# Weight-quarter sums of a Strassen-like MLP moved from VectorE to accumulating DMAs of GpSimd's queue

## The chip, the cores and the metric

The kernel runs on one core of a Trainium2 chip. The metric is the device time of one execution in microseconds (us); a median of several runs is given. A profile is one execution recorded by the hardware profiler, and the rows quoted below come from it. TensorE is called PE there, VectorE DVE, ScalarE ACT, GpSimd POOL, and SP is the engine from whose queue the loads are issued.

## What is computed

Two layers of a hybrid encoder work on 640 tokens (512 of a prompt, 128 of eight running streams) with a width of 1024. The part that matters here is the MLP at the end of each layer; its hidden width is 4096, and all is float32:

```python
h2 = rms_norm(x, ln2_w)
x = x + jnp.square(jax.nn.relu(h2 @ w_up)) @ w_down
```

## The kernel before

**Two-part products.** Every float32 operand of a matmul is split into a high and a low part, and a product is three matmuls (high by high, high by low, low by high). For a weight, ACT copies the raw floats into the reduced type (the high part, `weight_half` at L1119 to L1133), then DVE subtracts that from the raw floats (the low part, `weight_half` at L1772 to L1776).

**Seven products for eight.** The MLP is cut into four blocks of 1024 hidden features, in each layer. A block has an up stage and a down stage, so there are 16 such stages ("quads") in the two layers. In a quad the weights are a 2 by 2 arrangement of quarters, 11, 12, 21 and 22, each 512 by 512 floats (1 MB). Instead of the eight products of quarters for the prompt's tokens, seven products are made (a Winograd form of Strassen's scheme), with these weights, in this order: item 0 is 11, item 1 is 21, item 2 is 11 + 12, item 3 is 11 + 12 + 22, item 4 is 12 + 22, item 5 is 22, item 6 is 11 + 12 + 22 + 21. The code calls them B11, B21, SUM_1112, SUM_111222, SUM_1222, B22, SUM_ALL. The 128 stream tokens need plain products, which ride on items 0, 1, 4 and 5 (`up_sample`, `down_sample`): behind the item's own matmuls in general, but ahead of them for item 4, and in the down stage for item 5 too.

**Slots and ring.** The raw quarters lie in four 1 MB slots, `raws`. Each quarter is loaded once by a DMA from SP's queue (`load_quarter`, L453 to L457). The sums are made in place: DVE adds 12, then 22, then 21 onto the slot of 11, and 22 onto the slot of 12 (`weight_sum`, L1778 to L1798). An item has two halves, h0 and h1 of 512 KB each, and each half is summed, split and released by itself, so DVE makes 8 sums per quad. The split halves go into `ring`, which has room for two items: item n takes the place of item n - 2, half by half.

**Order.** Each engine works through a queue written out by hand. For item n, half h: ACT waits until PE is through with that half of item n - 2 and until the weight sum is there, and makes the high part; DVE makes the low part; PE waits for the low part. The next sum onto the same slot may only be made when DVE has read the slot for that low part. DVE's queue also holds the additions of PE's results into `x` (`add_to_x`, L1821), the sums of hidden parts (L1807), and the differences and low parts of the activations (`a_difference`, L1847 to L1856; `a_item_lo`, L1840). ACT's queue also holds copies from PSUM, ReLU and squares, and the high parts of the activations (L1221). In an up stage, two of these (`read_back`, L1195 and L1197) stand between the high parts of the two halves of item 4. GpSimd does nothing in the MLP beyond five small root computations ahead of it and two behind.

Of the kernel before, what the change touches and what calls it, by code (L numbers as in the profile page):

```python
# [17 lines left out]
DEPTH, D, TOK, SEQ, NB, NS = 2, 1024, 640, 512, 8, 16  # L18
P = 128
# [97 lines left out]
SLOTS = [(0, 1, 2, 3), (2, 3, 1, 0), (1, 0, 3, 2), (3, 2, 0, 1)]  # L117


def slot_of(quad, name):  # L120

    return SLOTS[quad % 4][("11", "12", "21", "22").index(name)]

# [3 lines left out]
SUMS = [(SUM_1112, 0), (SUM_1112, 1), (SUM_111222, 0), (SUM_111222, 1), (SUM_1222, 0), (SUM_1222, 1), (SUM_ALL, 0),  # L127
        (SUM_ALL, 1)]


def sums_to(quad, product, half):
    return quad * len(SUMS) + SUMS.index((product, half)) + 1

# [53 lines left out]
def program(nc, x_p, x_s, state_ret, state_conv, norm_rows, ln2_w, w_in, conv_w, ret_w, w_out, w_up, w_down,  # L187
# [6 lines left out]
    with ctx:  # L194
# [78 lines left out]
        sample_hidden = place("sample_hidden", [P, 2, 512], f32)  # L273
# [24 lines left out]
        tail = place("tail", [P, FT, 2 + 2 * NB], f32)  # L298
# [63 lines left out]
        slot_in = [Signal(f"slot_in{s}", 16 * QUADS) for s in range(4)]  # L362
# [3 lines left out]
        weights_summed = Signal("weights_summed", QUADS * len(SUMS))  # L366
# [72 lines left out]
        def settle(eng):  # L439


            eng.sem_inc(waits_passed, 1)
# [3 lines left out]
        def _(sp):  # L446
# [46 lines left out]
            with sp.Fori(0, DEPTH) as layer:  # L493
# [46 lines left out]
                for name in ("11", "21", "12", "22"):  # L540
                    load_quarter(layer, 0, name)
                sp.wait_ge(xn_ready.sem, xn_ready.at(layer, 2 * NT))
                load_norm_row(norm_rows, layer + 1)
                for quad in range(1, QUADS):
                    first = (quad - 1) * PRODUCTS
                    sp.wait_ge(weights_summed.sem, weights_summed.at(layer, sums_to(quad - 1, SUM_ALL, 1)))
                    settle(sp)
                    load_quarter(layer, quad, "11")
                    sp.wait_ge(half_lo.sem, half_lo.at(layer, 2 * (first + SUM_1222) + 2))
                    settle(sp)  # L550
                    load_quarter(layer, quad, "21")
                    sp.wait_ge(half_lo.sem, half_lo.at(layer, 2 * (first + B22) + 2))
                    settle(sp)
                    load_quarter(layer, quad, "12")
                    sp.wait_ge(half_lo.sem, half_lo.at(layer, 2 * (first + SUM_ALL) + 2))
                    settle(sp)
                    load_quarter(layer, quad, "22")
                sp.wait_ge(step_done.sem, step_done.at(layer, STEP["up", NBLK - 1, SUM_ALL, 1] + 1))
# [364 lines left out]
        def _(act):  # L923
# [89 lines left out]
            with act.Fori(0, DEPTH) as layer:  # L1013
# [105 lines left out]
                def weight_half(item, h):  # L1119
                    quad, i = divmod(item, PRODUCTS)  # L1120
                    if i in (B11, B21, B22):
                        slot = slot_of(quad, RAW_OF[i])
                        act.wait_ge(slot_in[slot].sem, slot_in[slot].at(layer, 16 * (quad + 1)))
                    else:
                        act.wait_ge(weights_summed.sem, weights_summed.at(layer, sums_to(quad, i, h)))
# [223 lines left out]
        def _(pool):  # L1349

# [80 lines left out]
            with pool.Fori(0, DEPTH) as layer:  # L1431
# [27 lines left out]
                for t in range(NT):  # L1459
                    row_rstd(layer, NT, t)  # L1460
                for p in range(2):
                    row_rstd(layer + 1, 0, p)
# [7 lines left out]
        def _(dve):  # L1470
# [173 lines left out]
            with dve.Fori(0, DEPTH) as layer:  # L1644
# [133 lines left out]
                def weight_sum(quad, i, h):  # L1778

                    a, b = {SUM_1112: ("11", "12"), SUM_111222: ("11", "22"), SUM_1222: ("12", "22"),  # L1780
                            SUM_ALL: ("11", "21")}[i]
                    if i == SUM_1112:
                        slot = slot_of(quad, "12")
                        dve.wait_ge(slot_in[slot].sem, slot_in[slot].at(layer, 16 * (quad + 1)))
                    elif i == SUM_111222:
                        slot = slot_of(quad, "22")
                        dve.wait_ge(slot_in[slot].sem, slot_in[slot].at(layer, 16 * (quad + 1)))
                    before = {SUM_1112: B11, SUM_111222: SUM_1112, SUM_ALL: SUM_111222}
                    if i in before:
                        dve.wait_ge(half_lo.sem, half_lo.at(layer, 2 * (quad * PRODUCTS + before[i]) + h + 1))  # L1790
                    if i == SUM_ALL:
                        dve.wait_ge(half_lo.sem, half_lo.at(layer, 2 * (quad * PRODUCTS + B21) + h + 1))
                    else:
                        n = SUMS.index((i, h)) + quad * len(SUMS)
                        if i in (SUM_111222, SUM_1222):
                            dve.wait_ge(weights_summed.sem, weights_summed.at(layer, sums_to(quad, SUM_1112, h)))
                    out = raw_half(quad, a, h)
                    nc.vector.tensor_tensor(out, out, raw_half(quad, b, h), ALU.add).then_inc(weights_summed.sem, 1)  # L1798

# [91 lines left out]
                def up(b):  # L1891
                    q, item = 2 * b, 2 * b * PRODUCTS
# [5 lines left out]
                    weight_sum(q, SUM_1112, 0)  # L1898
# [3 lines left out]
                    weight_sum(q, SUM_1112, 1)  # L1902
# [5 lines left out]
                    weight_sum(q, SUM_111222, 0)  # L1908
# [6 lines left out]
                    weight_sum(q, SUM_111222, 1)  # L1915
# [142 lines left out]
```

## Time and profile before

| | |
|---|---|
| median of 3 runs | 1522.8 us (1522.54 to 1523.48) |
| the profiled execution: time, span | 1517.21 us, 1515.4 us |
| PE busy, share of the span | 1433.9 us, 95% |
| DVE busy | 947.2 us, 63% |
| ACT busy | 593.2 us, 39% |
| POOL busy | 131.6 us, 9% |
| mean granted clock of PE | 0.979 |
| read from HBM | 115.83 MB |
| time that packets of SP's queue took, share of 16 DMA engines | 24.0% |

The span is what lies between the first and the last recorded instruction; the profiled execution's own time is 1.8 us more, and the median of the unprofiled runs is another 5.6 us more. Busy shares are averages over a whole program with stages of different kinds. What an edit is worth in the MLP is read from who waits for whom there.

### The profile page before, as it was taken

How to read it: one execution, taken by the hardware profiler on the slowest of the kernel's cores; microseconds unless marked ns; L12 is line 12 of the kernel's file. 1: busy time of each engine (PE TensorE's matmuls, PEld its weight loads, DVE VectorE, ACT ScalarE, POOL GpSimd, SP SyncE). 2: the span in 40 equal slices, each digit the busy share in tenths (PEclk: the TensorE clock that was granted, in tenths of full speed). 3: DMA queues.
4: the chain of work that ended last, by engine and by line, in shares of the span. 5: the costliest groups of instructions: out<-in, count | busy, mean ns of one | idle time of the engine just before them, and what ended most of it. 6: DMA issues, size and time to landing. Idle time of an engine off the chain costs nothing.

```text
span 1515.4 us, 22275 instructions
## 1 busy us (share of the span) xinstructions
PE 1433.9 (95%) x8198; PEld 1265.7 (84%) x8198; DVE 947.2 (63%) x1152; ACT 593.2 (39%) x743; POOL 131.6 (9%) x153
## 2 busy tenths in 40 slices
PE   8999999989899899899899999999899999999996
PEld 6888999889689788698688889988887887987985
DVE  6247335396866866867762562535877677677676
ACT  5212222264345345345442113214543543543553
POOL 2433000000000000000043330000000000000001
PEclk9999999999999999999999999999999999999998
DMA  7323111303203303304042221203113213203201
GB/s 254 126 84 113 63 56 57 112 15 112 96 17 112 111 1 112 111 16 153 2 148 97 88 81 63 93 25 121 72 41 111 73 40 111 84 28 112 87 26 70
DMA packets 74677, 124.72 MB, mean 82 GB/s; under 512 B 3332, under 2 KB 20868, under 8 KB 74568
## 3 DMA queue, kind: packets, MB, share of 16 engines
q1 hardware_dynamic: 74424, 123.18, 24.0%
q8 instruction: 70, 1.15, 0.3%
q14 instruction: 39, 0.32, 0.1%
q10 hardware_dynamic: 144, 0.07, 0.0%
HBM read 115.83 MB, written 7.41 MB: 81 GB/s over the span
## 4 chain that ended last, share of the span: by engine, by line
PE 77%; DVE 12%; issue 6%; ACT 4%; POOL 0%; DVEq 0%; DMA 0%; ACTq 0%; POOLq 0%
PE bank L612 22%; PE bank L770 15%; PE bank L622 11%; PE bank L863 11%; PE bank L784 7%; PE bank L876 5%; DVE raws L1798 4%; DVE ring L1775 3%; ACT ring L1132 3%; DVE x L1821 2%; PE bank L662 2%; DVE a_ring L1840 2%; PE bank L700 1%; PE bank L707 1%; PE bank L681 1%
## 5 line engine op out<-in xcount | busy, mean ns | idle before, releaser
L1132 ACT ACTIVATE ring<-raws 128x1024 fp32r<-128x1024 f32 x220 | 231.1, 1055 | 372.6 <-DVE raws L1798 124.3
L1775 DVE TENSOR_TENSOR ring<-raws,ring 128x1024 fp32r<-128x1024 f32 x220 | 268.8, 1222 | 169.2 <-ACT ring L1132 168.3
L863 PE MATMUL bank<-ring,a_ring 128*128 128x512 f32 x1344 | 318.1, 394 | 17.5 <-DVE a_ring L1840 17.5
L770 PE MATMUL bank<-mlp_in_hi,ring 128*128 128x256 f32 x1728 | 320.0, 283 | 0.0
L863 PEld LDWEIGHTS bank<-ring,a_ring 128*128 128x128 f32 x1344 | 254.1, 190 | 74.1 <-issue 20.8
L770 PEld LDWEIGHTS bank<-mlp_in_hi,ring 128*128 128x128 f32 x1728 | 272.1, 191 | 1.4
L770 PE MATMUL bank<-mlp_in_lo,ring 128*128 128x256 f32 x864 | 244.0, 282 | 0.0
L770 PEld LDWEIGHTS bank<-mlp_in_lo,ring 128*128 128x128 f32 x864 | 165.0, 191 | 1.4
L1798 DVE TENSOR_TENSOR raws<-raws 128x1024 f32<-128x1024 f32 x128 | 155.7, 1217 | 0.0
L1359 POOL TENSOR_SCALAR var<-sums 128x1 f32<-128x1 f32 x25 | 9.7, 386 | 1216.4 <-ACT xn L946 1212.8
L622 PE MATMUL bank<-norm_hi,ring 128*128 128x320 f32 x512 | 114.5, 310 | 0.0
L876 PE MATMUL bank<-ring,sample_mid_hi 128*128 128x512 f32 x256 | 88.6, 430 | 25.2 <-DVE ring L1775 25.2
L612 PE MATMUL bank<-ring,norm_hi 128*128 128x512 f32 x320 | 101.6, 399 | 4.2 <-ACT ring L934 2.3
L612 PE MATMUL bank<-pair_a,norm_hi 128*128 128x512 f32 x320 | 100.9, 397 | 0.0
L784 PE MATMUL bank<-ring,sample_in_hi 128*128 128x512 f32 x240 | 81.8, 424 | 18.7 <-DVE ring L1775 18.7
L1821 DVE TENSOR_TENSOR x<-x,bank 128x512 f32<-128x512 f32 x128 | 81.9, 679 | 19.7 <-PE bank L876 16.0
L876 PEld LDWEIGHTS bank<-ring,sample_mid_hi 128*128 128x128 f32 x256 | 53.1, 210 | 40.4 <-DVE ring L1775 28.6
L622 PEld LDWEIGHTS bank<-norm_hi,ring 128*128 128x128 f32 x512 | 86.0, 188 | 0.1
L622 PE MATMUL bank<-norm_lo,ring 128*128 128x320 f32 x256 | 79.1, 309 | 0.0
L612 PEld LDWEIGHTS bank<-ring,norm_hi 128*128 128x128 f32 x320 | 59.5, 191 | 16.4 <-ACT ring L934 2.5
L784 PEld LDWEIGHTS bank<-ring,sample_in_hi 128*128 128x128 f32 x240 | 47.2, 206 | 29.1 <-DVE ring L1775 20.3
L612 PEld LDWEIGHTS bank<-pair_a,norm_hi 128*128 128x128 f32 x320 | 58.9, 188 | 12.3 <-issue 1.0
(179 smaller groups left out, 2092.9 us busy)
## 6 DMA issues: line engine op xcount, KB each, us to landing
raws<-in_w_mlp_up SPq DMA_DIRECT2D x32, 1024.0 KB, 7.3
raws<-in_w_mlp_down SPq DMA_DIRECT2D x32, 1024.0 KB, 7.1
w_raw<-in_w_in SPq DMA_DIRECT2D x28, 1024.0 KB, 5.4
w_raw<-in_w_out SPq DMA_DIRECT2D x8, 1024.0 KB, 5.0
past_state<-in_state_ret SPq DMA_DIRECT2D x8, 512.0 KB, 5.1
out_ret_s<-past_state SPq DMA_DIRECT2D x8, 512.0 KB, 4.9
x<-in_x_prompt SPq DMA_DIRECT2D x4, 512.0 KB, 12.5
norm_row<-in_norm_rows SPq DMA_DIRECT2D x3, 512.0 KB, 3.6
```

The costliest lines, as they stand in the source:

```text
L612: mm = pe.matmul(out, act[a][:, k, tile * P:(tile + 1) * P], w_of(b, n), start=(n == 0 and m == 0), stop=(n == len(ks) - 1 and m == 2))
L622: mm = pe.matmul(out, w_of(chunk, k // 4, a)[:, k % 4, ft * P:(ft + 1) * P], norms[b][:, k, half * HALF:(half + 1) * HALF], start=(k == 0 ...
L662: mm = pe.transpose(out[:, i * P:(i + 1) * P], src[i], identity)
L770: mm = pe.matmul(cols, item_half(item, h, a)[:, k, n * P:(n + 1) * P], mlp_in[i][c][:, k], start=(i in (B11, B21, SUM_1112) and (n, k, m) ...
L784: mm = pe.matmul(out, x5[a][:, k], w[c][:, :, k], start=(i in (B11, SUM_1222) and (k, m) == (0, 0)), stop=(k == 3 and m == 2), skip_group_ ...
L863: mm = pe.matmul(out[:], a_item[:, a, 2 * h + k, pair * P:(pair + 1) * P], item_half(item, h, c)[:, k], start=(i in (B11, B21, SUM_1112) a ...
L876: mm = pe.matmul(sample_bank[:], sample_mid[part][a][:, k], item_half(item, k // 2, c)[:, k % 2], start=(i in (B11, SUM_1222) and (k, m) = ...
L1132: nc.scalar.activation(item_half(item, h, 0), raw_half(quad, RAW_OF[i], h), ACT.Copy).then_inc(half_hi.sem, 1)
L1775: nc.vector.tensor_tensor(item_half(item, h, 1), raw_half(quad, RAW_OF[i], h), f(item_half(item, h, 0)), ALU.subtract).then_inc(half_lo.se ...
L1798: nc.vector.tensor_tensor(out, out, raw_half(quad, b, h), ALU.add).then_inc(weights_summed.sem, 1)
L1821: nc.vector.tensor_tensor(xx, xx, src[:], op).then_inc(x_added.sem, 1)
L1840: nc.vector.tensor_tensor(a_ring[:, n % 2, 1], src, f(a_ring[:, n % 2, 0]), ALU.subtract).then_inc(a_lo.sem, 1)
```

## The change

DVE's 128 weight sums (8 per quad, 16 quads) are gone. For each of them GpSimd's queue issues a DMA that reads half a quarter from HBM and adds it onto the 512 KB already in the slot (`accum_op=ALU.add`). In an up stage the half is 128 partitions by 4 rows of 256 floats (runs of 1 KB), in a down stage by 2 rows of 512 floats (2 KB). SP still loads each quarter once; the adds are reads beside these. Before each add GpSimd waits until DVE has made the low part that reads the slot's former contents.

ACT now waits for the DMA's semaphore (`onto_11`, `onto_12`) where it waited for DVE's sum. The slots take turns otherwise: 11 alternates between slots 0 and 1, 21 and 22 share slot 2 one after the other, 12 always lies in slot 3; and SP's loads come in another order. The scratch space for descriptors of GpSimd's DMAs grows from 1024 to 2048 bytes, for which one small tile (`tail`) moves onto the place of another.

```diff
-                def weight_sum(quad, i, h):
...
-                    out = raw_half(quad, a, h)
-                    nc.vector.tensor_tensor(out, out, raw_half(quad, b, h), ALU.add).then_inc(weights_summed.sem, 1)
...
+                def add_onto(quad, i, name, h):
+
+                    src = (for_up, for_down)[quad % 2][bass.ds(layer, 1), quad // 2, int(name[0]) - 1, int(name[1]) - 1
+                                                       ].rearrange("l p k c -> (l p) k c")
+                    src = src[:, :, h * 256:(h + 1) * 256] if quad % 2 == 0 else src[:, 2 * h:2 * h + 2]
+                    done = onto_12[h] if i == SUM_1222 else onto_11[h]
+                    settle(pool)
+                    pool.dma_start(raw_half(quad, RAW_OF[i], h), src, accum_op=ALU.add).then_inc(done.sem, 16)
+
+                for quad in range(QUADS):
+                    for h in range(2):
+                        pool.wait_ge(half_lo.sem, half_lo.at(layer, 2 * (quad * PRODUCTS + B11) + h + 1))
+                        add_onto(quad, SUM_1112, "12", h)
+                    pool.wait_ge(slot_in[3].sem, slot_in[3].at(layer, 16 * slot_loads(quad, "12")))
+                    for h in range(2):
+                        add_onto(quad, SUM_1222, "22", h)
+                    for i, name in ((SUM_111222, "22"), (SUM_ALL, "21")):
+                        for h in range(2):
+                            before = ONTO_11[ONTO_11.index(i) - 1]
+                            pool.wait_ge(half_lo.sem, half_lo.at(layer, 2 * (quad * PRODUCTS + before) + h + 1))
+                            add_onto(quad, i, name, h)
...
+                    elif i == SUM_1222:
+                        act.wait_ge(onto_12[h].sem, onto_12[h].at(layer, 16 * (quad + 1)))
                     else:
-                        act.wait_ge(weights_summed.sem, weights_summed.at(layer, sums_to(quad, i, h)))
+                        act.wait_ge(onto_11[h].sem, onto_11[h].at(
+                            layer, 16 * (len(ONTO_11) * quad + ONTO_11.index(i) + 1)))
...
                 def down(b):
-                    q, item = 2 * b + 1, (2 * b + 1) * PRODUCTS
-                    weight_sum(q, SUM_1112, 0)
+                    item = (2 * b + 1) * PRODUCTS
                     weight_half(item + 1, 1)
...
-    nc = bacc.Bacc("TRN2", target_bir_lowering=False, num_devices=1, dynamic_dma_scratch_size=1024)
+    nc = bacc.Bacc("TRN2", target_bir_lowering=False, num_devices=1, dynamic_dma_scratch_size=2048)
```

On DVE, early in a down stage of the kernel before, from the additions into `x` of item 0 (L1821) on, stood this. L1798 is a weight sum, L1840 the low part of an activation, L1775 the low part of a weight (here item 2, h1), L1852 the difference that item 3's activation needs:

```order
L1821 TENSOR_TENSOR x<-x,bank 128x512 [waits step_done]
L1798 TENSOR_TENSOR raws<-raws 128x1024 [waits half_lo,slot_in2]
L1838 REGISTER_ALU
L1840 TENSOR_TENSOR a_ring<-diff,a_ring 128x1024 [waits a_hi]
L1796 REGISTER_ALU [waits half_lo,slot_in1]
L1798 TENSOR_TENSOR raws<-raws 128x1024 [waits weights_summed]
L1774 REGISTER_ALU
L1775 TENSOR_TENSOR ring<-raws,ring 128x1024 [waits half_hi]
L1852 SCALAR_TENSOR_TENSOR diff<-diff,hidden 128x1024 [waits a_lo]
```

At the same place of the changed kernel, whose lines have other numbers (L1831 is the addition into `x`, L1850 and L1807 the two low parts, L1862 the difference):

```order
L1831 TENSOR_TENSOR x<-x,bank 128x512 [waits step_done]
L1848 REGISTER_ALU
L1850 TENSOR_TENSOR a_ring<-diff,a_ring 128x1024 [waits a_hi]
L1806 REGISTER_ALU
L1807 TENSOR_TENSOR ring<-raws,ring 128x1024 [waits half_hi]
L1862 SCALAR_TENSOR_TENSOR diff<-diff,hidden 128x1024 [waits a_lo]
```

Both sums are gone from between these steps, and nothing takes their place.

On GpSimd nothing stood in a quad before. Now a down stage has these rows (L1479 is the add; a wait stands with the row ahead of the DMA or with the DMA). The first two DMAs add 12 onto 11, the next two 22 onto 12, the last two 22 onto 11:

```order
L1479 ISA [waits half_lo]
L1479 DMA raws<-in_w_mlp_down 128x2x512
L1483 REGISTER_ALU
L1479 ISA [waits half_lo]
L1479 DMA raws<-in_w_mlp_down 128x2x512
L1485 REGISTER_ALU
L1479 ISA [waits slot_in3]
L1479 DMA raws<-in_w_mlp_down 128x2x512
L1479 ISA
L1479 DMA raws<-in_w_mlp_down 128x2x512
L1491 REGISTER_ALU
L1479 DMA raws<-in_w_mlp_down 128x2x512 [waits half_lo]
```

The sums of a quad stand in one queue in this order, each pair behind the one before.

## Rows read from the trace of the kernel before

**Rows 1.** Waits of PE: engine, line, whom for; us in total, times, longest.
```profile
PE bank L876 <- DVE ring L1775: 25.2, 8, 3.6
PE bank L784 <- DVE ring L1775: 18.7, 8, 4.0
PE bank L863 <- DVE a_ring L1840: 17.5, 8, 2.2
```
**Rows 2.** Timeline of PE, one block: start, length, what, [idle before <- releaser].
```profile
673.81 0.72 PE L784 MATMUL bank<-ring,sample_in_hi 128*128 128x512 f32 x2 [1.78 <-DVE ring L1775]
...
721.21 5.07 PE L863 MATMUL bank<-ring,a_ring 128*128 128x512 f32 x14 [2.19 <-DVE a_ring L1840]
...
730.50 0.73 PE L876 MATMUL bank<-ring,sample_mid_hi 128*128 128x512 f32 x2 [1.95 <-DVE ring L1775]
```
**Rows 3.** Chain of work that ended last, same block: start, length, what.
```profile
730.50 4.41 PE bank L876 x12
...
740.57 2.80 PE bank L876 x12
743.37 5.48 PE bank L863 x24
```
**Rows 4.** Stretches: busy us and instructions per engine, PE clock, DMA share, GB/s.
```profile
719.50:725.00 5.50, 3.79 (x10) 2.98 (x11) 5.43 (x6) 2.61 (x3) 0.00 (x0) 0.69 0.00 0
...
688.30:691.00 2.70, 2.70 (x14) 2.21 (x13) 0.69 (x1) 0.00 (x0) 0.00 (x0) 1.00 1.05 386
```
**Rows 5.** Groups of instructions, DVE's weight sums: count | busy, mean ns | idle.
```profile
L1798 DVE TENSOR_TENSOR raws<-raws 128x1024 f32<-128x1024 f32 x128 | 155.7, 1217 | 0.0
```
**Rows 6.** Waits of ACT: us in total, times, longest.
```profile
ACT ring L1132 <- DVE raws L1798: 124.3, 54, 3.8
```
**Rows 7.** Timeline of ACT in the up stage of that block.
```profile
664.31 1.06 ACT L1132 ACTIVATE ring<-raws 128x1024 fp32r<-128x1024 f32 x1 [1.88 <-DVE raws L1798]
...
671.44 1.06 ACT L1132 ACTIVATE ring<-raws 128x1024 fp32r<-128x1024 f32 x1 [1.53 <-DVE raws L1798]
```
**Rows 8.** Timeline of DVE in the same up stage.
```profile
652.82 1.23 DVE L1775 TENSOR_TENSOR ring<-raws,ring 128x1024 fp32r<-128x1024 f32 x1 [5.39 <-ACT ring L1132]
654.25 1.23 DVE L1775 TENSOR_TENSOR ring<-raws,ring 128x1024 fp32r<-128x1024 f32 x1 [0.21 <-ACT ring L1132]
```
**Rows 9.** Timeline of ACT in the down stage of that block.
```profile
711.28 1.06 ACT L1132 ACTIVATE ring<-raws 128x1024 fp32r<-128x1024 f32 x1 [3.80 <-DVE raws L1798]
713.63 1.06 ACT L1132 ACTIVATE ring<-raws 128x1024 fp32r<-128x1024 f32 x1 [1.29 <-PE bank L876]
```
**Rows 10.** Timeline of DVE in the same down stage.
```profile
696.33 1.22 DVE L1775 TENSOR_TENSOR ring<-raws,ring 128x1024 fp32r<-128x1024 f32 x1 [2.91 <-ACT ring L1132]
...
706.55 1.23 DVE L1775 TENSOR_TENSOR ring<-raws,ring 128x1024 fp32r<-128x1024 f32 x1 [1.53 <-ACT ring L1132]
...
713.43 1.22 DVE L1775 TENSOR_TENSOR ring<-raws,ring 128x1024 fp32r<-128x1024 f32 x1
...
716.84 1.87 DVE L1821 TENSOR_TENSOR x<-x,bank 128x512 f32<-128x512 f32 x3
...
720.98 1.22 DVE L1775 TENSOR_TENSOR ring<-raws,ring 128x1024 fp32r<-128x1024 f32 x1
...
729.21 1.23 DVE L1775 TENSOR_TENSOR ring<-raws,ring 128x1024 fp32r<-128x1024 f32 x1
```
**Rows 11.** DMA issues: count, KB each, median us from issue to landing.
```profile
raws<-in_w_mlp_up SPq DMA_DIRECT2D x32, 1024.0 KB, 7.3
...
w_raw<-in_w_out SPq DMA_DIRECT2D x8, 1024.0 KB, 5.0
...
x<-in_x_prompt SPq DMA_DIRECT2D x4, 512.0 KB, 12.5
norm_row<-in_norm_rows SPq DMA_DIRECT2D x3, 512.0 KB, 3.6
```

More of the change, by code:

```diff
@@ L272, in program @@
         ret_state = place("ret_state", [P, H, HD], f32, ret_at + 2 * KB)
[L273 removed]
+        spare_at = region(4 * KB)
+        sample_hidden = place("sample_hidden", [P, 2, 512], f32, spare_at)
+        tail = place("tail", [P, FT, 2 + 2 * NB], f32, spare_at)
         at_of = {B11: norm_at, B21: norm_at + 8 * KB, SUM_1112: norm_at + 16 * KB, SUM_111222: temp_at,
@@ L361, in program @@
         group_done = Signal("group_done", PER_LAYER, start=1)
-        slot_in = [Signal(f"slot_in{s}", 16 * QUADS) for s in range(4)]
+        slot_in = [Signal(f"slot_in{s}", 16 * n) for s, n in enumerate((NBLK, NBLK, 2 * QUADS, QUADS))]
         step_done = Signal("step_done", len(STEPS), start=1)
@@ L365, in program @@
         half_lo = Signal("half_lo", 2 * ITEMS)
-        weights_summed = Signal("weights_summed", QUADS * len(SUMS))
+        onto_11 = [Signal(f"onto_11_{h}", 16 * len(ONTO_11) * QUADS) for h in range(2)]
+        onto_12 = [Signal(f"onto_12_{h}", 16 * QUADS) for h in range(2)]
         in_diff_hi = Signal("in_diff_hi", len(DIFFS) + 1)
@@ L539, in _ @@
                 settle(sp)
-                for name in ("11", "21", "12", "22"):
+                for name in ("11", "21", "12"):
                     load_quarter(layer, 0, name)
+                load_quarter(layer, 1, "11")
                 sp.wait_ge(xn_ready.sem, xn_ready.at(layer, 2 * NT))
                 load_norm_row(norm_rows, layer + 1)
[L544 to L555, printed above, removed]
+                for quad in range(QUADS):
+                    first = quad * PRODUCTS
+                    sp.wait_ge(half_lo.sem, half_lo.at(layer, 2 * (first + B21) + 2))
                     settle(sp)
                     load_quarter(layer, quad, "22")
+                    if quad < QUADS - 1:
+                        sp.wait_ge(half_lo.sem, half_lo.at(layer, 2 * (first + SUM_1222) + 2))
+                        settle(sp)
+                        load_quarter(layer, quad + 1, "12")
+                        sp.wait_ge(half_lo.sem, half_lo.at(layer, 2 * (first + B22) + 2))
+                        settle(sp)
+                        load_quarter(layer, quad + 1, "21")
+                    if quad < QUADS - 2:
+                        sp.wait_ge(half_lo.sem, half_lo.at(layer, 2 * (first + SUM_ALL) + 2))
+                        settle(sp)
+                        load_quarter(layer, quad + 2, "11")
                 sp.wait_ge(step_done.sem, step_done.at(layer, STEP["up", NBLK - 1, SUM_ALL, 1] + 1))
@@ L1460, in _ @@
                     row_rstd(layer, NT, t)
+                def add_onto(quad, i, name, h):
[5 more added lines that the diff above has]
+                    pool.dma_start(raw_half(quad, RAW_OF[i], h), src, accum_op=ALU.add).then_inc(done.sem, 16)
+                for quad in range(QUADS):
+                    for h in range(2):
[9 more added lines that the diff above has]
+                            add_onto(quad, i, name, h)
                 for p in range(2):
@@ L1891, in up @@
                 def up(b):
-                    q, item = 2 * b, 2 * b * PRODUCTS
+                    item = 2 * b * PRODUCTS
                     if b:
```

47 lines of the change are left out of this document (7 added, 40 removed).

## The prediction

> **What bounds the kernel now.** I read PE's waits first, then the timelines of one block of the second half of layer 0, from 632 to 743 us. PE is the bound, but it loses time in three places of each block: ahead of item 4 in the up stage, ahead of item 4 in the down stage (both times for a weight's low part), and ahead of item 3 in the down stage (for an activation's low part) [rows 1]. That is 25.2 + 18.7 + 17.5 = 61.4 us in the eight blocks of the two layers. In the block that I follow the three waits are 1.78, 2.19 and 1.95 us [rows 2]. The two in the down stage cost more than their length. Behind the first the granted clock is 0.69 over the next stretch [rows 4], that is, PE runs part of it at the lower of its two levels: item 3 takes from 721.21 to 728.55 (730.50 less the wait of 1.95), 7.34 us, where an undisturbed item of the stage takes 5.48 [rows 2, 3]. Behind the second the stream tokens' 12 matmuls take 4.41 us where they take 2.80 undisturbed [rows 3]. So the clock costs 1.9 + 1.6 = 3.5 us a block, 28 us in eight, and all that could be won in the MLP is 61 + 28 = 89 us.
>
> Behind all three waits stands DVE, and in its queue the weight sums: 128 of 1217 ns, 155.7 us [rows 5]. ACT stands still 124.3 us in 54 waits for them [rows 6].
>
> **What the change removes.** The 155.7 us of DVE are not themselves on the path; what counts is where two or three of them stand between steps that PE waits for. I replay the block with the sums gone, and with the landing time L of an add (from the semaphore that lets GpSimd go to the full count) left open. Only the adds of 22 onto 11 for item 3 are tight, since the low part that frees the slot (item 2) is made one item ahead; the other pairs have two items or more.
>
> *Up stage.* Item 2's low part of h1 ends at 654.25 + 1.23 = 655.5 [rows 8]; then the add may go. Before, ACT's split of item 3, h1 began at 664.31, 1.88 late for a sum, and the split of item 4, h1 at 671.44, 1.53 late for another; PE started item 4 at 673.81 [rows 2, 7]. From the first of these to PE's start are 9.5 us; without the 1.53 it is a string of 8.0. PE is through with item 3 at 673.81 - 1.78 = 672.0. The wait is gone if the h1 add lands by 672.0 - 8.0 = 664.0, that is if L is at most 8.5 us. Between 8.5 and 10.3 it comes back, above 10.3 this place is later than before, by as much as L is longer. Gain below 8.5: all 18.7 us of that row [rows 1]; I count nothing for the clock there.
>
> *Down stage, h0.* Item 2's low part of h0 ends at 706.55 + 1.23 = 707.8 [rows 10]. ACT split item 3, h0 at T = 713.63, when PE had freed the ring [rows 9]. Behind that split, 1.06, stand on DVE the low part, 1.22, three additions into x, 1.87, and item 3's activation, 1.22, some 5.6 us with the handing over; the sum that stood there too is gone. PE could start item 3 at 719.2, and it is through with item 2 at 721.21 - 2.19 = 719.0. If the add lands after 713.6, T is 707.8 + L.
>
> *Down stage, h1.* Item 2's low part of h1 began at 713.43, behind two sums that go [rows 10], as the order of DVE shows: it now ends near 713.43 - 2.3 + 1.22 = 712.4. ACT's split of that half stood 3.80 us for one of these sums [rows 9]; it is ready in time. The add lands at 712.4 + L, the split ends 1.1 later, and then DVE goes through the low part of item 3, h1, and all up to the low part of item 4, h1. Before, that string ran from 720.98 to 729.21 + 1.23 = 730.4 [rows 10], 9.5 us with two sums in it, so 7.2 now. It ends at 720.7 + L, and before at 730.4: the break-even is L = 9.7 us. With L below 5.6 DVE's own pace takes over, and it ends at 719.1 + 7.2 = 726.3.
>
> **What L is.** No row shows an accumulating DMA or one of GpSimd's queue. The bounds are rows of SP's loads [rows 11]. The shortest like it is a 512 KB copy, 3.6 us; it reads half of what an add must read (512 KB from HBM and 512 KB from the slot). A 1 MB load reads as much: 5.0 us where it runs alone, 7.3 for the MLP's quarters, which are issued close behind each other. The longest row is the 512 KB of x, 12.5 us in a crowd. I take 7.3: the adds go to the same slots, come in pairs, and run beside the quarters' loads. [...]
>
> **The sum at L = 7.3.** Up: the wait goes, 18.7 us. Down: h0 lands at 715.1, item 3 starts at 720.7, after a wait of 1.7. Item 4's low part is ready at 720.7 + 7.3 = 728.0 where it was at 730.4: 2.4 us sooner, and with the clock left as it was (one wait of the two is still near 2 us) 8 x 2.4 = 19 us. Together 38 us, plus a little in the blocks whose wait was 3.6 rather than 1.95 [rows 1]; I take 40. The profiled execution would go from 1517.2 to 1477; the median lies 5.6 above it, so 1483. PE's matmuls do not change. SP's loads stay at 64; each waits for a low part and lands one item or more ahead of need, which costs nothing. GpSimd's root computations stand ahead of and behind the adds, and wait for events that come after the last item is split: nothing.
>
> **What crowds.** At 386 GB/s, a share of 1.05 [rows 4], 1 MB occupies the DMA engines for 2.7 us. Per block the adds read as much as 16 such loads, 43 us, beside 8 loads, 22 us: 65 of the block's 111 us, where 22 were. In the down stage, the second add for item 2 may only start at 696.33 + 1.22 = 697.6 [rows 10], and two adds for item 4 and the load of 22 come right behind: four times 2.7 is 10.8 us, until 708.4, so that item 3's h0 add, due at 707.8, finds the engines just free. With a wait of 1 us there the gain of the down stage shrinks by at most 8 us; this is in the range.
>
> **Rivals.**
> *A, the adds are quick (L near 5).* Speaks for it: the lone 1 MB load, 5.0. Down: item 3's wait goes (719.2 against 719.0), item 4 at 726.3, 4.1 us sooner, and up to 1.6 to 3.5 more where the clock stays up. 18.7 + 8 x 4.1 = 51, up to 79: 1444 to 1472.
> *B, the adds are slow: a wait for a sum by DMA takes the place of the wait for a sum by DVE.* The place is ACT's split of item 3, h1, in both stages; it decides from L = 9.7 (down) and 10.3 (up). For it: pairs go through one queue, behind the two adds for item 4, and an add reads and writes the slot; the 12.5 us row shows what a crowd does. At 12.5: up 2.2 later than before, down 12.5 - 9.7 = 2.8 later; 8 x 5.0 = 40 us more, 1563. The break-even band, L of 9.6 to 10.0, gives no measurable change.
> *C, GpSimd or the DMA engines become the bound.* 16 adds a block have 111 us, less 22 for the loads: 89 / 16 = 5.6 us of all DMA engines each, or 6.9 us of GpSimd each to write their descriptors (512 runs of 1 KB in the up stage). Nothing in the trace prices either. At 8 us each a block takes 128 us instead of 111: 8 x 17 = 136 us, 1659. The same kernel whose engines would be 59% busy by the copy's price is over 100% if an add costs twice that. [...]
> *D, the change does not do what it says:* if adds of a pair are held up behind the wait for slot 3 in GpSimd's queue, sums come late for another reason than their own length. The quarter 12 is loaded three items ahead, so I give it no share of its own.
>
> **How the numbers follow.** The forecast, L from 6 to 9.4: 0.38, with 1470 to 1515. A: 0.13. The band without measurable change (a measurement of this kernel can tell about 0.2%, 3 us, from none): 0.06. B: 0.25, 1526 to 1590. C: 0.18, from 1560 upward. Faster is 0.38 + 0.13 = 0.51, slower 0.25 + 0.18 = 0.43. For 8 in 10 the range goes from 1455, which leaves out the quick half of A (0.06), to 1600, which leaves out three quarters of C (0.13).
>
> **What would show it.** In the changed kernel's profile DVE's busy time is 156 us less (right under every case). The DMA issue rows give L. Under the forecast, PE's wait ahead of the up stage's item 4 is gone, those ahead of the down stage's items 3 and 4 are still there but shorter, and ACT's waits for DVE's sums are replaced by fewer for DMA. Under B, ACT waits longest for a DMA at item 3, and PE behind it; under C every pair of adds is late, item 2's and item 4's too, the DMA share or GpSimd's issue time is near full, and the loss grows evenly over the quads. The prediction is wrong if L is above 9.7, or if the first pair's adds already come late.

## The result and the profile after

The changed kernel took 1620.8 us, median of four runs (1617.5 to 1622.1), against 1522.7 for the kernel before in the same rounds: 1.065 times as long, 95% interval 1.062 to 1.068. The forecast was 1483, the range 1455 to 1600, with 0.51 for faster. It is slower by 98 us and lies above the range.

Lines of the page of the kernel after: the busy us of each engine with share of the span and instructions, the DMA queues (packets, MB, share of 16 engines), and the DMA issues:

```profile
span 1615.6 us, 22559 instructions
...
PE 1440.9 (89%) x8198; PEld 1274.2 (79%) x8198; DVE 803.4 (50%) x1024; ACT 591.0 (37%) x743; POOL 292.2 (18%) x281
...
q0 software_dynamic: 51200, 67.12, 26.7%
q1 hardware_dynamic: 74424, 123.18, 23.1%
...
raws<-in_w_mlp_up POOLq DMA_DIRECT2D x64, 512.0 KB, 6.5
raws<-in_w_mlp_down POOLq DMA_DIRECT2D x64, 512.0 KB, 5.8
```

DVE lost 144 us of work (947.2 to 803.4), not the 156 that I had said: a sum's row is 1.22 us long, but the next row begins 1.13 us after its start (at 710.03 and 711.16 in the kernel before), busy time counts the overlap once, and 128 times 1.13 is 145. The adds land in 6.5 and 5.8 us at the median, counted from their issue, both under the 7.3 I had taken from [rows 11] and below the break-even. And yet the kernel is slower. The waits of PE (who, for whom, us in total, times, longest), to be held against [rows 1]:

```profile
PE bank L797 <- ACT sample_hidden L1190: 107.0, 8, 19.5
PE bank L868 <- DVE a_ring L1850: 19.4, 8, 4.0
PE bank L789 <- DVE ring L1807: 16.6, 8, 2.9
PE bank L775 <- DVE ring L1807: 7.5, 6, 1.6
...
PE bank L881 <- DVE ring L1807: 4.2, 5, 1.0
```

One row is new and holds the loss: 107.0 us in eight waits, one in each up stage, ahead of the turn of the stream tokens' hidden part. All five make 154.7 us where [rows 1] has 61.4, 93 more; PE's busy time is 7 us longer (1433.9 to 1440.9), and 93 + 7 is the 100 us by which the span grew. The wait for a weight ahead of the down stage's item 4 fell from 25.2 to 4.2 us, as meant.

What PE waits for is a square on ACT, and that stands in ACT's queue behind the high part of item 3's first half. PE's row in the block of [rows 2], whose up stage begins 42 us later in this execution (at 685 instead of 643 us), ACT's row, DVE's low part of item 2's first half, and then GpSimd's rows of that up stage:

```profile
720.04 1.11 PE L797 MATMUL bank<-const,sample_hidden 128*128 128x128 f32 x4 [12.09 <-ACT sample_hidden L1190]
```

```profile
717.78 1.06 ACT L1140 ACTIVATE ring<-raws 128x1024 fp32r<-128x1024 f32 x1 [19.18 <-DMA raws<-in_w_mlp_up]
```

```profile
694.84 1.23 DVE L1807 TENSOR_TENSOR ring<-raws,ring 128x1024 fp32r<-128x1024 f32 x1 [7.28 <-ACT ring L1140]
```

```profile
680.24 1.28 POOL L1479 DMA_DIRECT2D raws<-in_w_mlp_up  x1 [21.00 <-DVE ring L1807]
687.14 1.30 POOL L1479 DMA_DIRECT2D raws<-in_w_mlp_up  x1 [5.61 <-issue]
697.78 1.29 POOL L1479 DMA_DIRECT2D raws<-in_w_mlp_up  x1 [9.35 <-issue]
704.26 1.30 POOL L1479 DMA_DIRECT2D raws<-in_w_mlp_up  x1 [5.18 <-issue]
711.10 1.29 POOL L1479 DMA_DIRECT2D raws<-in_w_mlp_up  x1 [5.54 <-issue]
717.99 1.30 POOL L1479 DMA_DIRECT2D raws<-in_w_mlp_up  x1 [5.60 <-issue]
724.64 1.29 POOL L1479 DMA_DIRECT2D raws<-in_w_mlp_up  x1 [5.34 <-issue]
```

Issuing an add keeps GpSimd busy for 1.3 us, and then it mostly stands still for 5.2 to 5.6 us, for nothing that a semaphore explains ("issue"). The adds of this up stage go out 6.5 to 6.9 us apart, which is their landing time: each goes when the one before has landed (the one of 704.26 after 6.5 us, at 710.8; the next row starts at 711.10). The one longer gap, 10.6 us behind the second add, fits too: SP issued the load of a quarter beside it, and it landed only at 697.5, after 10.4 us, when ACT's split that waited for it began. In a down stage they go out close behind each other:

```profile
756.16 3.67 POOL L1479 DMA_DIRECT2D raws<-in_w_mlp_down  x3 [2.99 <-DVE ring L1807]
```

Three in 3.67 us. So the add that item 3's first half needs, the fifth in the queue, goes out at 711.10, 15 us after item 2's low part let it go (DVE made that from 694.8 to 696.1), and lands at 717.8, 21.7 us after it could have gone. While one add is under way the DMA engines are half idle (share 0.54 in two stretches of 6.8 us):

```profile
704.20:711.00 6.80, 3.75 (x32) 3.55 (x30) 0.00 (x0) 0.00 (x0) 1.30 (x1) 0.95 0.54 77
711.10:717.90 6.80, 0.00 (x0) 0.00 (x0) 0.00 (x0) 0.12 (x1) 1.29 (x1) 0.50 0.54 77
```

**Theory R:** the descriptors of two up-stage adds do not fit in the scratch space of 2048 bytes, so GpSimd has to see the first drained before it can write the second; three of the down stages' fit. **Rival G:** GpSimd needs that long to make the descriptors of 512 runs. **Rival E:** the DMA engines need that long for runs of 1 KB.

### The profile page after: what moved, and what is told of

Read it like the earlier page. It is cut to its first block, busy times and chain, and to the rows that moved or that the text cites. A ratio compares the mean times of both kernels' runs of the same rounds, so it can differ in the third digit from the quotient of the medians.

```text
span 1615.6 us, 22559 instructions
## 1 busy us (share of the span) xinstructions
PE 1440.9 (89%) x8198; PEld 1274.2 (79%) x8198; DVE 803.4 (50%) x1024; ACT 591.0 (37%) x743; POOL 292.2 (18%) x281
## 4 chain that ended last, share of the span: by engine, by line
PE 62%; issue 21%; DMA 7%; DVE 5%; ACT 4%; POOL 1%; POOLq 0%; ACTq 0%; DVEq 0%
PE bank L617 20%; PE bank L627 10%; PE bank L868 9%; PE bank L775 9%; PE bank L881 4%; DMA raws<-in_w_mlp_down 4%; DMA raws<-in_w_mlp_up 3%; PE bank L789 3%; DVE ring L1807 3%; ACT ring L1140 2%; PE bank L667 2%; DVE x L1831 1%; PE bank L705 1%; PE bank L712 1%; PE bank L686 1%
## 5 line engine op out<-in xcount | busy, mean ns | idle before, releaser
L1807 DVE TENSOR_TENSOR ring<-raws,ring 128x1024 fp32r<-128x1024 f32 x220 | 268.5, 1224 | 406.8 <-ACT ring L1140 406.3
L1140 ACT ACTIVATE ring<-raws 128x1024 fp32r<-128x1024 f32 x220 | 231.3, 1056 | 480.0 <-DMA raws<-in_w_mlp_up 213.0
L775 PE MATMUL bank<-mlp_in_hi,ring 128*128 128x256 f32 x1728 | 335.0, 291 | 7.5 <-DVE ring L1807 7.5
L868 PEld LDWEIGHTS bank<-ring,a_ring 128*128 128x128 f32 x1344 | 255.6, 191 | 76.3 <-issue 22.7
L775 PEld LDWEIGHTS bank<-mlp_in_hi,ring 128*128 128x128 f32 x1728 | 284.6, 199 | 10.3 <-DVE ring L1807 8.7
L775 PE MATMUL bank<-mlp_in_lo,ring 128*128 128x256 f32 x864 | 250.3, 290 | 0.0
L775 PEld LDWEIGHTS bank<-mlp_in_lo,ring 128*128 128x128 f32 x864 | 172.1, 199 | 1.4
L1479 POOL DMA_DIRECT2D raws<-in_w_mlp_up x64 | 83.2, 1300 | 457.8 <-issue 325.5
L1479 POOL DMA_DIRECT2D raws<-in_w_mlp_down x64 | 77.3, 1339 | 327.5 <-DVE ring L1807 327.5
L797 PE MATMUL bank<-const,sample_hidden 128*128 128x128 f32 x64 | 13.7, 353 | 107.0 <-ACT sample_hidden L1190 107.0
L797 PEld LDWEIGHTS bank<-const,sample_hidden 128*128 128x128 f32 x64 | 9.4, 179 | 108.6 <-ACT sample_hidden L1190 108.6
L1831 DVE TENSOR_TENSOR x<-x,bank 128x512 f32<-128x512 f32 x128 | 82.2, 683 | 19.7 <-PE bank L881 16.0
L881 PE MATMUL bank<-ring,sample_mid_hi 128*128 128x512 f32 x256 | 79.9, 393 | 4.2 <-DVE ring L1807 4.2
```

Source lines behind the costliest of these rows:

```text
L775: mm = pe.matmul(cols, item_half(item, h, a)[:, k, n * P:(n + 1) * P], mlp_in[i][c][:, k], start=(i in (B11, B21, SUM_1112) and (n, k, m) ...
L797: mm = pe.transpose(back_bank[:, j * P:(j + 1) * P], sample_hidden[:, n, j * P:(j + 1) * P], identity)
L868: mm = pe.matmul(out[:], a_item[:, a, 2 * h + k, pair * P:(pair + 1) * P], item_half(item, h, c)[:, k], start=(i in (B11, B21, SUM_1112) a ...
L881: mm = pe.matmul(sample_bank[:], sample_mid[part][a][:, k], item_half(item, k // 2, c)[:, k % 2], start=(i in (B11, SUM_1222) and (k, m) = ...
L1140: nc.scalar.activation(item_half(item, h, 0), raw_half(quad, RAW_OF[i], h), ACT.Copy).then_inc(half_hi.sem, 1)
L1479: pool.dma_start(raw_half(quad, RAW_OF[i], h), src, accum_op=ALU.add).then_inc(done.sem, 16)
```

## Experiments

### e1, e2, e3 and m1: room, the two kinds of stage, and the adds alone

e1 changes one number of the changed kernel:

```diff
-    nc = bacc.Bacc("TRN2", target_bir_lowering=False, num_devices=1, dynamic_dma_scratch_size=2048)
+    nc = bacc.Bacc("TRN2", target_bir_lowering=False, num_devices=1, dynamic_dma_scratch_size=2112)
```

> The changed kernel with 64 bytes more descriptor scratch per partition (2112 instead of 2048), nothing else. Theory R (room): in the changed kernel's trace the adds of an up stage are issued 6.65 us apart, each when the one before has landed, while those of a down stage go out three in a row 1.2 us apart; the reason is that the descriptors of two up-stage adds do not fit in the scratch together and those of three down-stage adds do. [...] R expects the up-stage adds to go out in pairs, the longest wait of PE (107.0 us ahead of the turn of the stream tokens' hidden part) to shrink below 30 us, and a time of 1500 to 1550 us. Rival G (GpSimd makes 512 runs' descriptors in 5 to 6 us that the trace does not show as busy) and rival E (the DMA engines need 6.65 us for an add of 1 KB runs): the 6.65 us spacing stays and the time is 1615 to 1625 us.

**1484.2 us, 0.976 of the kernel before (0.972 to 0.979).** 64 bytes per partition are worth 137 us. GpSimd's rows of an up stage and PE's waits in e1:

```profile
629.27 1.30 POOL L1479 DMA_DIRECT2D raws<-in_w_mlp_up  x1 [21.01 <-DVE ring L1807]
632.11 1.29 POOL L1479 DMA_DIRECT2D raws<-in_w_mlp_up  x1 [1.53 <-DVE ring L1807]
635.87 1.30 POOL L1479 DMA_DIRECT2D raws<-in_w_mlp_up  x1 [2.47 <-issue]
639.16 1.29 POOL L1479 DMA_DIRECT2D raws<-in_w_mlp_up  x1 [1.99 <-issue]
```

```profile
PE bank L868 <- DVE a_ring L1850: 19.3, 8, 4.3
PE bank L797 <- ACT sample_hidden L1190: 15.5, 2, 7.8
...
PE bank L881 <- DVE ring L1807: 3.9, 4, 1.0
PE bank L789 <- DVE ring L1807: 3.0, 4, 1.1
```

The adds now go out 2.8 to 3.8 us apart, two under way at a time, and the 107.0 us are 15.5, in two waits. R foretold the pairs and the shrunken wait; the time is lower than the 1500 to 1550 expected. G and E foretold no change. I chose 2112 by an estimate of mine of the descriptors that an add needs; no run shows their number or their size. What the traces show is one up-stage add under way at a time with 2048 bytes, and two with 2112: in e1 the third goes out at 635.87, when the first, of 629.27, has landed after 6.3 us.

e2 is the kernel before with adds for the down stages' sums alone, e3 the mirror. Both carry a table of the sums made by adds (up stages first), from which the wait of the splitting engine, DVE's sums and GpSimd's adds follow:

```diff
+BY_DMA = [(), (SUM_1112, SUM_111222, SUM_1222, SUM_ALL)]
...
+                    if i in BY_DMA[quad % 2]:
+                        return
```

> The kernel before, where only the 64 weight sums of the down stages are made by GpSimd's accumulating DMAs; the 64 of the up stages stay on VectorE. The slots take turns as in the kernel before. Theory R expects the loss to lie in the up stages only: a down stage took 44.6 us in the changed kernel where it took 46.1 before (one block), so 8 x 1.5 = 12 us less or somewhat more, 1500 to 1515 us. If an add of any form is too slow, the time is above 1526 us.

> The mirror of e2: only the up stages' 64 sums are made by accumulating DMAs, with 2048 bytes of scratch. Theory R: an up stage took 69.9 us in the changed kernel and 54.0 before (one block), so the whole loss and 10 to 20 us more than the changed kernel's, 1620 to 1650 us. If the two kinds of stage share the loss: 1570 us.

**e2: 1487.4 us, 0.978 (0.975 to 0.982). e3: 1645.3, 1.082 (1.078 to 1.085).** e2 did better than expected, 35 us less than before, not 12. The expectation came from one block, which was not like the others: PE's wait ahead of item 4 was 1.95 us there before, where six of the eight blocks had 3.5 or more, and in the changed kernel its wait ahead of item 3 was 4.0, where the other seven had 1.8 to 2.5 (at that time SP loads the next layer's weights). e3 has the whole loss, in the range expected, and its longest wait of PE is the same one, 105.8 us in eight times. Down stages alone win 35, up stages alone lose 123. Both kernels keep the slots' turns and the order of loads of the kernel before, so the new ones are not what makes the loss.

m1 takes the adds out of the kernel: GpSimd alone, 512 KB each, 2048 bytes of scratch.

```diff
+            for form in ("up", "down"):
+                for accumulate in (True, False):
+                    for n in range(8):
+                        add(form, n, n, accumulate)
+                    wait_all()
```

> The disputed cost by itself; nothing of the reference is computed. GpSimd issues, with nothing else running and 2048 bytes of scratch: 8 adds in the up stages' form (4 runs of 1 KB per partition, 512 KB), 8 plain copies in that form, 8 adds and 8 copies in the down stages' form (2 runs of 2 KB), then 4 single adds of each form, each waited for. Theory R: up-form adds land one after the other, some 5 to 6.7 us apart, with the DMA engines about half busy; up-form copies and down-form adds go out two to three in flight, below 3.5 us apart. Rival E: the up-form adds' spacing is filled by the DMA engines (share near 1). Rival G: GpSimd's issue rows are 5 us apart for up-form copies too.

Its rows on GpSimd, first for the up-form adds, then for the same form as plain copies (L43), then for the down-form adds:

```profile
26.97 1.43 POOL L41 DMA_DIRECT2D slots<-in_w_mlp_up  x1 [26.52 <-DVEq L13]
33.46 1.31 POOL L41 DMA_DIRECT2D slots<-in_w_mlp_up  x1 [5.06 <-issue]
39.78 1.29 POOL L41 DMA_DIRECT2D slots<-in_w_mlp_up  x1 [5.01 <-issue]
...
78.70 2.29 POOL L43 DMA_DIRECT2D slots<-in_w_mlp_up  x3 [5.47 <-DMA slots<-in_w_mlp_up]
...
96.23 3.66 POOL L41 DMA_DIRECT2D slots<-in_w_mlp_down  x3 [5.18 <-DMA slots<-in_w_mlp_up]
```

The up-form adds go out 6.3 to 6.5 us apart with nothing else on the core, so neither the kernel's own loads nor DVE is behind it. Copies of the very same 512 runs go out three in 2.29 us, which speaks against G. The DMA share over the eight up-form adds was 0.58, which speaks against E.

### e4, e5, e6 and m2: more room, another order, fewer adds

m2 is m1 with 16384 bytes of scratch.

> The same as m1 with 16384 bytes of descriptor scratch; nothing of the reference is computed. Theory R: the 8 up-form adds, 6.4 us apart in m1, are issued 1.3 us apart now, and land 3.3 to 3.6 us apart (what their descriptors occupy of the DMA engines); down-form adds 1.2 and about 3 us. Rivals G and E: 6.4 us apart as before.

```profile
26.95 10.62 POOL L41 DMA_DIRECT2D slots<-in_w_mlp_up  x8 [26.51 <-DVEq L13]
52.99 5.97 POOL L43 DMA_DIRECT2D slots<-in_w_mlp_up  x8 [15.42 <-DMA slots<-in_w_mlp_up]
```

All eight adds are issued in 10.62 us, 1.3 each, which settles G. They have landed by 52.99, 26.0 us after the first was issued, where m1 took 51.7 (26.97 to 78.70). That is 3.25 us per add with the DMA engines full (share 0.98 from 27 to 60 us), the first one's latency included, just under the 3.3 to 3.6 expected: the price in throughput that my prediction had put at 2.7. The eight down-form adds took 24.7 us, 3.1 each. E is refuted for the 6.65 us.

e5 gives the changed kernel 4160 bytes. In its trace three up-stage adds are under way at a time (issued from 626.09 to 631.45; the fourth goes out at 632.67, when the first has landed after 6.3 us):

```diff
-        spare_at = region(4 * KB)
-        sample_hidden = place("sample_hidden", [P, 2, 512], f32, spare_at)
+        spare_at = region(2 * KB)
+        sample_hidden = [place(f"sample_hidden{n}", [P, 512], f32, (temp_at + 8 * KB, spare_at)[n]) for n in range(2)]
...
-    nc = bacc.Bacc("TRN2", target_bir_lowering=False, num_devices=1, dynamic_dma_scratch_size=2112)
+    nc = bacc.Bacc("TRN2", target_bir_lowering=False, num_devices=1, dynamic_dma_scratch_size=4160)
```

> [...] Theory R: with two in flight the room is no longer what PE waits for, except in each layer's first up stage, where the adds start late: 1475 to 1484 us, GpSimd's idle time before an add that no semaphore explains falls from 82.9 to below 40 us. If the adds' pace is still set by room: below 1470 us.

**1477.7 us, 0.971 (0.969 to 0.974).** In the expected band, with 47.5 us of unexplained idle on GpSimd rather than the less than 40 expected (82.9 in e1). Beyond two adds, room is worth some 6 us at most; the intervals of e1 and e5 just overlap.

e4 issues the pair for item 4 ahead of the pair for item 2:

```diff
                 for quad in range(QUADS):
+                    pool.wait_ge(slot_in[3].sem, slot_in[3].at(layer, 16 * slot_loads(quad, "12")))
+                    for h in range(2):
+                        add_onto(quad, SUM_1222, "22", h)
                     for h in range(2):
...
-                    pool.wait_ge(slot_in[3].sem, slot_in[3].at(layer, 16 * slot_loads(quad, "12")))
-                    for h in range(2):
-                        add_onto(quad, SUM_1222, "22", h)
```

> Kernel of e1 (2112 bytes of scratch), with the pair of adds that makes 12 + 22 (needed for item 4) issued ahead of the pair for item 2 instead of behind it; nothing else. Theory Q (queue and crowd): what is left of the wait ahead of the down stage's item 3 (19.3 us in eight waits in e1) comes from the item-3 adds landing late, because three adds and a load go out right ahead of them; with two of the three moved forward they land 1 to 2 us sooner: 1468 to 1480 us, that wait below 12 us. Rival D: that wait is made by VectorE's own queue or by the add's own 5.8 us; then the time stays within 3 us of e1's 1484.2.

**1482.1 us, 0.973 (0.971 to 0.976),** not to be told apart from e1, whose interval overlaps. The wait that it was made for did shrink, from 19.3 to 7.9 us, below the 12 of the expectation, so the crowd ahead of item 3's adds is real; but each layer's first up stage got a wait of up to 8.9 us in its place, since item 2's adds now stand behind two more, and PE waits 9.8 us, not 3.9, for item 4 of the down stages. The time expected (down to 1468) was a miss.

e6 leaves the tight sums on DVE: adds make those for items 4 and 6 alone, in all stages, with 2112 bytes of scratch. It is built on the kernel before and keeps its slots' turns.

```diff
+BY_DMA = [(SUM_1222, SUM_ALL), (SUM_1222, SUM_ALL)]
```

> The kernel before, where in every stage the sums for items 4 and 6 (12 + 22, and 21 onto the rest) are made by accumulating DMAs, and those for items 2 and 3 stay on VectorE; 2112 bytes of scratch. No add is then tight. Theory: the waits ahead of both item 4s shrink by the two sums that stood in VectorE's string (2.3 us each), the one ahead of the down stage's item 3 stays near 17 us: 1475 to 1492 us, as good as e1 with half the adds. Rival: the sums for items 2 and 3 are what hurts; then above 1500 us.

**1461.0 us, 0.960 (0.958 to 0.962):** half of the adds win 61 us, more than all of them with room for two did (38, e1), and more than expected. PE's waits in e6:

```profile
PE bank L884 <- DVE a_ring L1888: 17.5, 8, 2.2
...
PE bank L805 <- DVE ring L1823: 3.1, 2, 1.6
...
PE bank L897 <- DVE ring L1823: 2.1, 2, 1.0
```

The waits ahead of both item 4s are gone but for 5.2 us, and the one for item 3's activation is [rows 1] to the digit. The profiled e6 is 24 us shorter than e1's. PE's waits give 19 of these and its busy time 5. Of the 19, some 14 lie in each layer's first up stage (17.5 us of waits there in e1, 3.1 in e6). So most of what e6 has over e1 is not the tight adds themselves but the late start of a layer's first adds, to which e10 comes back.

### e7 to e10: the same scarcity elsewhere, and what is left

e7 asks whether the loss can be moved into the down stages: e2 with half the room.

```diff
-    nc = bacc.Bacc("TRN2", target_bir_lowering=False, num_devices=1, dynamic_dma_scratch_size=2048)
+    nc = bacc.Bacc("TRN2", target_bir_lowering=False, num_devices=1, dynamic_dma_scratch_size=1024)
```

> Kernel of e2 (only the down stages' sums by accumulating DMAs, 1487.4 us) with 1024 instead of 2048 bytes of descriptor scratch. [...] Theory R expects the loss of the changed kernel to appear in the down stages: adds issued 5.5 to 6 us apart, one at a time; a down stage has 8 adds, 46 us of its 46, so it becomes as late as the up stages were: 1530 to 1600 us. If the slowness belongs to the 1 KB runs and not to room, the time stays at 1487.

**1576.4 us, 1.038 (1.035 to 1.041),** 89 us over e2. The down-stage adds, which had gone out three in a row:

```profile
604.93 1.22 POOL L1492 DMA_DIRECT2D raws<-in_w_mlp_down  x1 [4.79 <-issue]
610.79 1.21 POOL L1492 DMA_DIRECT2D raws<-in_w_mlp_down  x1 [4.64 <-issue]
616.88 1.22 POOL L1492 DMA_DIRECT2D raws<-in_w_mlp_down  x1 [4.87 <-issue]
```

Some 6.0 us apart, with runs of 2 KB; the one of 604.93 had landed after 5.5. The cause is room for descriptors, not the form of the add. If adds share the scratch evenly, the runs alone bound what one takes: an up-stage add more than 1024 bytes (one fits in 2048) and at most 1056 (two in 2112), a down-stage add more than 512 (one in 1024) and at most 682 (three in 2048).

e8 makes one more sum of e6 by adds, that for item 2 in the down stages; e9 adds a swap on DVE.

```diff
-BY_DMA = [(SUM_1222, SUM_ALL), (SUM_1222, SUM_ALL)]
+BY_DMA = [(SUM_1222, SUM_ALL), (SUM_1112, SUM_1222, SUM_ALL)]
```

```diff
-                    weight_sum(q, SUM_111222, 1)
                     a_item_lo(b, SUM_111222)
+                    weight_sum(q, SUM_111222, 1)
```

> Kernel of e6 (1461.0 us) where in the down stages the sums for item 2 too are made by adds; VectorE makes those for items 2 and 3 in the up stages and for item 3 in the down stages. Theory: PE's last steady wait, 17.5 us in eight waits ahead of the down stage's item 3, hangs on VectorE's string, out of which one 1.14 us step goes ahead of the split that decides: the waits fall to 7 to 10 us, with their clock cost partly, 1440 to 1456 us. Rival: this wait hangs on what frees the ring, and stays; 1458 to 1463 us.

> Kernel of e8, with two neighbours swapped on VectorE in the down stage: the low part of item 3's activation ahead of the sum for item 3, h1. Theory: another 1.14 us less ahead of item 3's activation; the wait falls below 3 us in all, the clock stays up in the down stages: 1425 to 1440 us. Rival: the sum that is now later delays item 3's second half by as much; the same as e8.

**e8: 1453.5 us, 0.956 (0.953 to 0.959), the fastest kernel here. e9: 1468.4, 0.965 (0.962 to 0.968): a miss, 15 us slower where it should have been faster.** PE's waits in e8, then in e9:

```profile
PE bank L884 <- DVE a_ring L1888: 9.6, 8, 1.2
PE bank L897 <- DVE ring L1823: 8.3, 8, 1.1
```

```profile
PE bank L897 <- DVE ring L1823: 21.7, 8, 2.7
...
PE bank L884 <- DVE ring L1823: 2.4, 8, 0.3
```

The swap did move the wait: item 3's is down to 2.4 us, and item 4's grew, since the delayed sum delays the split of item 3's second half and DVE's string behind it (DVE stands still 1.12 us for that split in the block below, at 490.9, and not at all in e8). The waits together are only some 6 us more (24.1 against 17.9); the rest is the clock. The stream tokens' matmuls ahead of item 4 in one down stage of e8 (a wait of 1.03 before them), and the same place in e9 (a wait of 2.70), as stretches with PE's busy time first and the granted clock third from the end:

```profile
495.70:498.80 3.10, 3.07 (x13) 2.55 (x14) 3.10 (x4) 1.04 (x2) 0.00 (x0) 1.00 0.56 114
```

```profile
499.00:505.00 6.00, 5.95 (x14) 4.70 (x15) 4.59 (x5) 0.00 (x0) 0.00 (x0) 0.50 0.66 189
```

Twelve matmuls took 3.0 us with the clock at 1.00 (495.73 to 498.75) and 5.5 at 0.50 (499.05 to 504.54). PE's busy time is 1409.7 us in e8 and 1421.9 in e9: 12 us more for the same matmuls. In e8 the clock is 1.00 over the 3 us behind each of its down stages' sixteen waits, which are 1.0 to 1.2 us long, so they cost their length. In e9 it is 0.50 to 0.60 behind six of the eight waits of 2.7 us, and 1.00 behind the other two: such a wait mostly costs the clock as well.

e10 is e1 with each layer's first pair of adds issued earlier:

```diff
-                for t in range(NT):
+                for t in range(3):
                     row_rstd(layer, NT, t)
...
                         add_onto(quad, SUM_1112, "12", h)
+                    if quad == 0:
+                        for t in range(3, NT):
+                            row_rstd(layer, NT, t)
```

> Kernel of e1 (1484.2 us), where in each layer GpSimd issues the first stage's pair of adds for item 2 after the third of the five root computations instead of behind the fifth. Theory F: the two waits of 15.5 us in all ahead of the turn of the stream tokens' hidden part are those of the two first up stages, whose adds start 10 to 12 us late because they stand behind roots that wait for ScalarE's squares; both waits fall below 3 us each, 1468 to 1477 us. Rival: they come from the crowd of DMAs at the layer's start; unchanged within 3 us.

**1473.2 us, 0.970 (0.967 to 0.972),** 11 us under e1, as expected. Of the 15.5 us in two waits 1.2 are left, and 7.5 in place of 3.0 stand ahead of the up stages' item 4.

## Why the prediction was wrong

**The step that failed** is the use of L as the only price. I replayed item 3's add as if it went out the moment its semaphore came, with the adds ahead of it only sharing the DMA engines (the paragraph on what crowds). In fact an add also takes up a third resource, the descriptor scratch, and in the up stages two do not fit in its 2048 bytes (they go out one landing time apart, and two at a time with 2112). The fifth add of the queue went out 15 us late. Its landing, counted from the semaphore as my L is, came after 21.7 us, far above the 8.5 that I had allowed the second half of item 3 in the up stage. PE lost 107.0 us to it in eight waits, and 64 bytes more gave back 137 us (e1). The diff showed a change of exactly this resource, from 1024 to 2048 bytes, and I named it without asking how many adds it has room for.

**The place** was not in the replay either. I followed the second half of item 3; PE lost its time for the first half, since the square for the stream tokens stands behind that split in ACT's queue. PE was there at 707.95 (720.04 less 12.09), and from ACT's split to PE's start are 2.26 us, so this add had to land by 705.7: my estimate is that L may be 9.6 us there.

**What bounds the kernel** was right in the main. With DVE relieved, PE's waits in the MLP fell from 61.4 us to 41.7 in e1 (15.5 of them new) and to 22.7 in e6. Of the three, those ahead of the item 4s went; the one ahead of item 3 stayed (19.3 in e1, where the add's landing takes the place of DVE's sums), and shrank only in e4, e8 and e9. The clock's part was near in sum, but by luck: PE's busy time is 1433.9 us before and 1409.7 in e8, 24 us, where I had 28. But I multiplied one block by eight. Over the 3 us behind the wait ahead of item 3, always 2.19 us long, the granted clock was below 1.00 in two blocks of eight only (0.57 and 0.56), mine among them; behind the one ahead of item 4, in all eight (0.50 to 0.73). In the up stage, where I had counted nothing, it was below 1.00 in five of eight (0.50 to 0.61). The block itself runs from 643 to 754 us and not from 632 to 743.

**L.** I took 7.3 us. The medians from issue to landing are 6.5 and 5.8, but a median over all adds is not what counts. The tight add for item 3's first half in a down stage of e1 took 7.2 us (issued at 382.46, ACT's split at 389.62), and 9.3 in the last block of the first layer, where SP loads the next layer's weights: near the break-even of 9.7.

**The forecast's mechanism, with room for two adds,** gives 1484.2 us (e1) where the forecast was 1483. That they agree is in part luck, as misses cancel. The up stage's wait went (18.7 to 3.0 us) and item 3's in the down stage stayed near 2 us (2.11 in one block, 1.7 forecast). But item 4's fell below 1 us where I had left it near 2: the 1.95 us of my block were 3.5 or more in six blocks, for which "a little" was too little. Against that, the first up stages lost 15.5 us.

**GpSimd's root computations** I had counted at nothing. They stand ahead of each layer's first adds, and e10 shows 11 us for it. A queue that an operation is moved onto delays the operation by what already stands in it.

**The cases.** C, to which I gave 0.18, is the nearest by its numbers: it was to set in where adds follow each other by 6.9 us, and in the up stages they went out some 6.65 us apart. Its causes did not come about: GpSimd was busy 1.3 us of the 6.65, the DMA engines were half idle, and the loss lay in the up stages alone. By its shape it is D, sums held up in GpSimd's queue for another reason than their own length, to which I gave no share, since I thought of slot 3 only. B did not happen: even the slowest tight add in e1, 9.5 us in that same block, is below the break-even, though PE's wait there is 4.3 us. In C, an add at twice the copy's price would make the DMA engines 97% busy (86 and 22 of 111 us), not over 100%; at the 3.25 us that m2 shows it is two thirds.

**The range** reached 1600, and the time is 21 us above it. Above it I had left only three quarters of C, 0.13, and nothing for a hold-up in the queue.

## What to carry to other kernels

An add that GpSimd's queue issues takes room for descriptors as well as time on the DMA engines: of the up-stage form one was under way at a time with 2048 bytes of scratch, two with 2112 (e1), three with 4160 (e5), and eight went out in a row with 16384 (m2). Before laying out how many must be under way, let a small kernel such as m1 show how many the room holds. Here 64 bytes too few halved the number, and the trace shows it as DMAs issued one landing time apart (6.5 to 6.9 us), with idle time on the issuing engine that no semaphore explains (5.2 to 5.6 us each) and a half-idle DMA share (0.54).

Move to another engine the work that is not tight, and leave the tight link where it is: PE's wait ahead of the down stage's item 3 is 17.3 us with all of that stage's sums made by adds (e2), and 9.6 with item 3's left on DVE (e8). See also what stands in the queue already that takes the work: here roots ahead of each layer's first adds, 11 us (e10). And two short waits of PE can be cheaper than one long one, because of the clock: it stayed at 1.00 behind waits of 1.0 to 1.2 us (e8) and was 0.50 to 0.60 behind six of the eight of 2.7 us (e9).

## What the runs showed that I had not expected

- 64 bytes of scratch per partition changed the time from 1620.8 to 1484.2 us.
- Accumulating costs GpSimd 1.3 us per 512 runs of 1 KB where a copy of the same runs costs some 0.76 (2.29 us for three), and 1.2 for 256 runs of 2 KB. An add of 512 KB lands 5.8 to 6.6 us after its issue at the median in the changed kernel and e1 (7.9 for the up stages' in e8, 9.3 for one in a crowd), and eight in a row land 3.25 us apart in the 1 KB form (m2).
- Waits of 1.0 to 1.2 us left PE's granted clock at 1.00 in sixteen cases of sixteen (e8). Waits of 2.19 us were followed by less in two of eight (0.57 and 0.56; before, ahead of item 3), those of 2.7 in six of eight (0.50 to 0.60; e9).
- The best version found, 1453.5 us, is 4.4% faster than the kernel before (interval 4.1 to 4.7%). It leaves on VectorE the sums for items 2 and 3 in the up stages and for item 3 in the down stages.
- Left open: whether all sums by adds would do as well as e6 or e8 with the 4160 bytes of e5 and the early first adds of e10, and whether e8 would gain from more room; no run has these together.
